# Last query block, page loads and weight splits: reordering around the attention of a two-layer decoder step

## What is computed

```
layer 0: h += hgrn2_mixer(rmsnorm(h)) @ w_o0 ;  h += conv_ffn(rmsnorm(h))
k, v, logf = shared_kv(h)           # keys and values of 16 heads of 64
layer 1: q, gate = split(rmsnorm(h) @ w_qg) ; q = rmsnorm(q) per head
         prompt:  p = softmax(q k^T / 8 + c_q - c_k, causal)        # 512 x 512 per head
         samples: the same over 512 cached keys (4 pages of 128) and the 8 new ones
         h += (p v * sigmoid(gate)) @ w_o1 ;  h += conv_ffn(rmsnorm(h))
```

## Time and profile before

| | |
|---|---|
| median of 3 runs | 1701.38 us (1699.66 to 1705.09) |
| profiled execution | 1702.34 us, its span 1700.8 us |
| TensorE busy | 1629.9 us, 96% |
| VectorE / ScalarE / GpSimd busy | 851.9 / 616.7 / 303.1 us |
| mean granted TensorE clock | 0.981 of full speed |

### The profile page before, as it was taken

The page is one execution under the profiler, slowest core; times in us unless marked ns, Lnnn a source line. Parts: engine busy times, 40 slices in busy tenths (PEclk is TensorE's granted clock), DMA queues, the critical chain, the costliest instruction groups (busy, mean ns, idle before and its releaser), DMA issues.

```text
span 1700.8 us, 36540 instructions
## 1 busy us (share of the span) xinstructions
PE 1629.9 (96%) x14346; PEld 1554.1 (91%) x14346; DVE 851.9 (50%) x1498; ACT 616.7 (36%) x978; POOL 303.1 (18%) x363
## 2 busy tenths in 40 slices
PE   5999999979999999999999999888899999999997
PEld 5998989959999999999999999655699999999997
DVE  5666666644555555433343443566455555554221
ACT  4444334423333333322233354556334333333111
POOL 3222222212222222100100100122022222221000
PEclk8999999989999999999999999999999999999999
DMA  4222222212222222222233334388422222223330
GB/s 171 64 90 83 74 88 77 79 40 87 85 81 86 77 83 80 86 84 80 85 114 114 117 107 146 106 320 312 179 87 89 77 84 86 75 85 93 99 99 30
DMA packets 51879, 174.41 MB, mean 103 GB/s; under 512 B 6914, under 2 KB 8338, under 8 KB 51778
## 3 DMA queue, kind: packets, MB, share of 16 engines
q1 hardware_dynamic: 46850, 155.83, 27.7%
q0 software_dynamic: 4928, 17.12, 2.8%
HBM read 160.36 MB, written 12.57 MB: 102 GB/s over the span
## 4 chain that ended last, share of the span: by engine, by line
PE 71%; issue 3%; DVE 2%; ACT 1%; DMA 1%; SPq 0%; POOL 0%; DVEq 0%; ACTq 0%; POOLq 0%
PE acc L1450 66%; DMA dec_B<-c_samp 1%; PE aux L1631 1%; PE aux L1697 1%; PE aux L1752 1%; PE aux L1710 1%; PE acc L1729 1%; PE acc L1680 0%; ACT att_Pr L694 0%; SPq L374 0%; DVE w_lo L779 0%; PE aux L1494 0%; DVE att_Pr L1169 0%; ACT w_hi L433 0%; DVE acc L1156 0%
## 5 line engine op out<-in xcount | busy, mean ns | idle before, releaser
L1450 PE MATMUL acc<-xl,w_hi 128*128 128x288 f32 x2192 | 489.6, 305 | 23.4 <-DVE w_lo L779 14.7
L1450 PE MATMUL acc<-xh,w_lo 128*128 128x288 f32 x2192 | 473.6, 298 | 0.0
L1450 PE MATMUL acc<-xh,w_hi 128*128 128x288 f32 x2192 | 473.4, 298 | 0.0
L779 DVE TENSOR_TENSOR w_lo<-w_raw,w_hi 128x1024 fp32r<-128x1024 f32 (+1 forms) x217 | 283.6, 1307 | 331.9 <-ACT w_hi L433 330.4
L1450 PEld LDWEIGHTS acc<-xl,w_hi 128*128 128x128 f32 x2192 | 356.6, 191 | 35.2 <-DVE w_lo L779 15.4
L1450 PEld LDWEIGHTS acc<-xh,w_hi 128*128 128x128 f32 x2192 | 357.4, 191 | 0.0
L1450 PEld LDWEIGHTS acc<-xh,w_lo 128*128 128x128 f32 x2192 | 357.1, 191 | 0.0
L433 ACT ACTIVATE w_hi<-w_raw 128x1024 fp32r<-128x1024 f32 (+1 forms) x217 | 224.4, 1034 | 268.3 <-PE acc L1450 235.4
L1450 PE MATMUL acc<-ffn_glo,w_hi 128*128 128x288 f32 x704 | 151.3, 296 | 0.0
L1450 PE MATMUL acc<-ffn_gh,w_lo 128*128 128x288 f32 x704 | 150.0, 293 | 0.0
L1450 PE MATMUL acc<-ffn_gh,w_hi 128*128 128x288 f32 x704 | 149.1, 293 | 0.0
(11 more groups left out here) (241 smaller groups left out, 2102.9 us busy)
## 6 DMA issues: line engine op xcount, KB each, us to landing
w_raw<-w_fi_in SPq DMA_DIRECT2D x88, 512.0 KB, 3.3
w_raw<-w_mix_in SPq DMA_DIRECT2D x32, 512.0 KB, 3.3
w_raw<-w_fo_in SPq DMA_DIRECT2D x32, 512.0 KB, 3.5
dec_Kd<-cache_k_in SPq DMA_DIRECT2D x32, 512.0 KB, 5.8
att_Vd<-cache_v_in SPq DMA_DIRECT2D x32, 512.0 KB, 5.8
w_raw<-w_kv_in SPq DMA_DIRECT2D x17, 512.0 KB, 3.4
w_raw<-w_o_in SPq DMA_DIRECT2D x16, 512.0 KB, 3.3
w_raw<-w_qg_in SPq DMA_DIRECT2D x16, 512.0 KB, 3.3
```

Of the source, the lines that this page charges most:

```text
L779: nc.vector.tensor_tensor(w_lo[:, pos.slot % SPL, 0:width], w_raw[:, pos.slot, 0:width], w_hi[:, pos.slot % SPL, 0:width].bitcast(F32), AL ...
L1450: mm = nc.tensor.matmul(acc[:, tp, hf, 0:HALF], W[:, sp_, 128 * (j0 + j):128 * (j0 + j) + 128], X[:, kt, HALF * hf:HALF * hf + HALF], star ...
```

## The change

- **Splits.** In the `w_o0`/`w_o1` loop of `ffn`, `hi` and `lo` of block m+2 are done in round m: on ScalarE ahead of the tile's square and `xh`, on VectorE between `add_h` and `gain_lo`.
- **First scores.** `score(0, 0)` is issued within the last gate block, after its third k-tile. VectorE does its two `mx`, `inverse` and `scale_p` ahead of the scaling of gate tile 7; ScalarE does its two `ex` within `key_norm` of query tile 7.
- **Late norm.** `key_gain` of query tile 7 stands behind `mx` of tile 1 in round 0; the gate logarithm of tile 7 comes later, after `ex` of tile 1. In round 0 `turns(0, 0)` stands ahead of `score(0, 1)`.
- **Memory.** `Kd` changes places with `Pr` and `PT`. So the key pages of sample 0 are loaded only when block 140 is done, behind the loads of `w_o1` blocks 0 to 3.
- **Block 142.** Its `hi` and `lo` move from round 0 to the end of round 7.
- **End.** `sample_scores(7)` comes after round 7, `turns(7, 2)` and `sample_turn(6)` are in round 7 and no longer within the first `w_o1` block; `sample_max(7)` and `sample_exp(7)` move behind round 7.

```diff
         t3 = Region("dec", x_at)
-        Kd = t3("Kd", [P, PAGES, 8 * P])
+        Pr = t3("Pr", [P, 2, 2, SEQ])
+        PT = t3("PT", [P, 2, 2, NCH, P])
...
         t4 = Region("att")
-        Pr = t4("Pr", [P, 2, 2, SEQ])
-        PT = t4("PT", [P, 2, 2, NCH, P])
+        Kd = t4("Kd", [P, PAGES, 8 * P])
...
             sample_bias(0)
-            key_pages(0)
             for j in range(4):
                 load(Pos(B_WO1 + j), d["w_o1"][j])
             sp.wait_ge(block_done, B_WO1)
+            key_pages(0)
             value_pages(0)
...
                 for m in range(DT):
-                    if m:
-                        hi(Pos(b_in - 8 + m + 1))
+                    hi(Pos(b_in - 8 + m + 2))
                     out_tile(m, n_h0 + m + 1, None, s_base + m, G_FFN + 8 * layer)
-                hi(Pos(b_in + 1))
...
                 if split is not None:
                     hi(split)
+                if between is not None:
+                    between()
                 act.wait_ge(km_ps, n + 1)
...
+            def first_ex():
+                ex(0, 0, 0)
+                ex(0, 0, 1)
             qg_pair(0, 6, 3, 4)
-            qg_pair(1, 7, 3, 4, True)
+            qg_pair(1, 7, 3, 4, True, first_ex)
...
                     ex(i, 1, 1)
+                    if not prev:
+                        gate_log_of(7)
                     ex(i, 2, 0)
                     ex(i, 3, 0)
...
-                    ex(3, 1)
-                    if not prev:
-                        hi(Pos(B_WO1 + 1))
+                    ex(i, 3, 1)
                 if i == NSEQ - 1:
-                    sample_exp(i)
+                    hi(Pos(B_WO1 + 1))
...
                 for m in range(DT):
-                    if m:
-                        lo(Pos(b_in - 8 + m + 1))
                     add_h(m, b_in - 8 + m, (t_in - 8 + m) % 2, h_base + m + 1)
+                    lo(Pos(b_in - 8 + m + 2))
                     gain_lo(xl, xh, m, G_FFN + 8 * layer, x_base + m)
-                lo(Pos(b_in + 1))
...
                 lo(Pos(B_QG + 2 + 2 * k, i, step))
+                if last is not None:
+                    last()
                 scaled(tile_of(GT, p), b + 1, (T_QG + 1) % 2, gx_ok)
...
+            def first_max():
+                mx(0, 0, 0)
+                mx(0, 0, 1)
+                inverse(0, 0, 1)
+                scale_p(0, 0, 0)
+                inverse(0, 1, 2)
+                scale_p(0, 0, 1)
...
                     mx(i, 1, 0)
                     mx(i, 1, 1)
                     if not prev:
-                        gate_logsig(7)
+                        key_gain(QT, 7, 15, gq[:, 0:1])
...
+            def first_score():
+                pe.wait_ge(kn_ok, 9)
+                score(0, 0)
...
                 if more:
                     pe.wait_ge(kn_ok, 16)
                     score(i + 1, 0)
-                else:
-                    sample_scores(i)
                 pv(i, 1)
-                if more:
-                    turns(i, 2)
-                    if prev:
-                        sample_turn(i - 1)
-            pe.wait_ge(kn_ok, 9)
-            score(0, 0)
+                turns(i, 2)
+                if prev:
+                    sample_turn(i - 1)
+            qg_pair(0, 6, 3, 4)
+            qg_pair(1, 7, 3, 4, {2: first_score})
             for i in range(NSEQ):
                 att(i)
             e = NSEQ - 1
-
-            def end_turns():
-                turns(e, 2)
-                sample_turn(e - 1)
+            sample_scores(e)
             pe.wait_ge(ex_ok, 8 * NSEQ)
             gemm(Pos(B_WO1), T_WO1, T_WO1 % 2, range(DT), ah, al, wait_x=(al_ok, 0), part=True, hfs=(0,),
-                 mid={0: end_turns, 2: lambda: pv(e, 2), 4: lambda: sample_turn_p(e)})
+                 mid={0: lambda: pv(e, 2), 4: lambda: sample_turn_p(e)})
```

More of the change, by code:

```diff
@@ L612, in _, with key_norm @@
             ffn(0, B_FI0, B_FO0, G_KV, 1, 0, 8)
-            def key_norm(src, p, n, split=None):
+            def key_norm(src, p, n, split=None, between=None):
                 act.wait_ge(kr_ok, n + 1)
@@ L666, in gate_exp, with qg_pair @@
                 nc.scalar.activation(tile_of(GT, p), tile_of(GT, p), ACT.Exp).then_inc(gt_ok, 1)
-            def qg_pair(k, p, i, step, last=False):
+            def qg_pair(k, p, i, step, last=False, between=None):
                 if isinstance(p, int) and p == 0:
@@ L672, in qg_pair @@
                 hi(Pos(B_QG + 2 + 2 * k, i, step))
-                key_norm(QT, p, p + 8, None if last else Pos(B_QG + 3 + 2 * k, i, step))
+                key_norm(QT, p, p + 8, None if last else Pos(B_QG + 3 + 2 * k, i, step), between)
                 if not last:
@@ L756, in att @@
                     gated_hi(i - 1)
+                    if not cur:
+                        sample_copy(i - 1)
                 else:
@@ L1110, in _, with qg_pair @@
             dve.wait_ge(gq_ok, 1)
-            def qg_pair(k, p, i, step, last=False):
+            def qg_pair(k, p, i, step, last=None):
                 b = B_QG + 2 * p
@@ L1125, in qg_pair @@
                 nc.vector.sem_inc(evac, 1)
-                if not last:
+                if last is None:
                     lo(Pos(B_QG + 3 + 2 * k, i, step))
-                key_gain(QT, p, p + 8, gq[:, 0:1])
-                if not last:
+                    key_gain(QT, p, p + 8, gq[:, 0:1])
                     gate_logsig(p)
@@ L1141, in _, with mx @@
                 qg_pair(1, 2 * i + 1, i, 4)
+            def mx(i, s, a):
+                x, w, at = tile_no(s, a), P * (NCH - s), tile_at(s)
+                dve.wait_ge(sc_ps, 3 * i + min(s, 2) + 1)
+                dve.wait_ge(msk_ok, 4 * i + (1, 3, 4, 4)[s])
+                nc.vector.sem_inc(taking, 1)
+                sc = acc[:, unit_bank(i, min(s, 2)), a, at:at + w]
+                bias = NC[:, i % 2, a, 0:w] if s < 3 else NC0[:, a, :]
+                nc.vector.tensor_tensor_reduce(out=sc, in0=sc, in1=bias, scale=-1.0, scalar=3.0e38,
+                                               op0=ALU.add, op1=ALU.min, accum_out=nm[:, x:x + 1]).then_inc(mx_ok, 1)
@@ L1142, in _ @@
+            def first_max():
[5 more added lines that the diff above has]
+                scale_p(0, 0, 1)
             qg_pair(0, 6, 3, 4)
-            qg_pair(1, 7, 3, 4, True)
+            qg_pair(1, 7, 3, 4, first_max)
             def att(i):
                 cur, prev = i < NSEQ, i > 0
[L1149 to L1167, removed]
-                    pr = Pr[:, n % 2, a, at:at + w]
-                    nc.vector.tensor_scalar(pr, pr, rr[:, x:x + 1], None, ALU.mult).then_inc(pn_ok, 1)
@@ L1216, in gate_sample @@
                     last.then_inc(dgo_ok, 1)
-                if cur:
-                    mx(0, 0)
-                    mx(0, 1)
-                    inverse(0, 1)
-                    scale_p(0, 0)
-                    if prev:
-                        sample_max(i - 1)
-                    inverse(1, 2)
-                    scale_p(0, 1)
+                if cur and prev:
+                    mx(i, 0, 0)
+                    mx(i, 0, 1)
+                    inverse(i, 0, 1)
+                    scale_p(i, 0, 0)
+                    sample_max(i - 1)
+                    inverse(i, 1, 2)
+                    scale_p(i, 0, 1)
+                if not cur:
+                    sample_max(i - 1)
                 if prev:
@@ L1765, in att @@
                     pv(i - 1, 2)
-                score(i, 1)
-                if not prev:
+                    score(i, 1)
+                    turns(i, 0)
+                else:
                     pe.wait_ge(kln_ok, 16)
-                turns(i, 0)
+                    turns(i, 0)
+                    score(i, 1)
                 score(i, 2)
```

85 lines of the change are left out of this document (45 added, 40 removed).

## The result

| | before | after |
|---|---|---|
| median beside each other, 5 runs each | 1702.41 us | 1690.82 us (1690.10 to 1692.34) |
| ratio, 95% interval | | 0.993 (0.9916 to 0.9945) |
| profiled execution, its span | 1702.34, 1700.8 us | 1692.34, 1690.8 us |

The forecast was 1692.0, in a range of 1687 to 1697.5, and "faster" at 0.84, with 0.3% as the bound; the whole interval of the ratio lies beyond it. The profiled execution of the changed kernel is the slowest of its five, 1.5 us over their median. It is 10.0 us shorter than the one before.

A forecast was written before the change was run, and what follows sets the result against it. TensorE, busy 96% of the span, was taken as the bound, so only its idle or slow spells could give. 3.0 + 1.3 + 2.0 + 3.5 = 9.8 us off 1702.34 or median 1701.38; forecast 1692.0, range 1687 to 1697.5.

The forecast's parts named there:

- Part 1a: Change-over into `w_o0`: splits first let block 34 start 2.0 us sooner, 1.0 less slow clock; 3.0 us (2.0 to 4.7).
- Part 1b: Layer 1's `w_o1` loop, before block 143: earlier splits remove TensorE's idle time; 1.3 us, lower end 1.0.
- Part 2: Into attention: moved halves of block 142 and first scores let `turns(0,2)` go sooner; 2.0 us, 0.3 to 2.9.
- the head start is used up: Into attention: late `key_gain` and the third mask hold `mx(0,2)` until 1087.6, against 1087.5 before.
- Part 3: End of attention: `pv(7,1)` and `turns(7,2)` run during the wait for `sample_scores(7)`; 3.5 us, 1.9 to 5.0.
- the two small waits: End of attention, new order: about 1.2 us until the copy of `turns(7,1)`, and 0.34 for the scaling before `turns`.
- A: Key pages land late, `sample_scores(0)` waits, all gain into attention goes; sum 7.8 us, or 1693.8; chance 0.12.
- B: End of attention gives only 0.5 us: clock drops again, value pages replace key pages; sum 6.8, or 1694.8; chance 0.09.
- C: Two more slow stretches at other moments in attention, each up to 1.65 us; sum 6.5, or 1695; chance 0.07.
- D: Masks and gate work hold `turns(0,2)`, attention's end waits as before; both attention gains are nothing, 1697.2; chance 0.06.
- E: Attention loop: late bias row brings three more 3.4 us stalls plus slow stretches, costing 15.2 us; 1707.7; chance 0.04.

The follow-up runs named there:

- run 2: Kernel before with only block 142's `hi` and `lo` moved from round 0 to the end of round 7: 1698.0 us, ratio 0.9982.
- run 10: Changed kernel with the old end of attention put back, measured again beside the changed kernel: 1691.7 us, ratio 0.9945 to before.
- runs 3 and 11: Changed kernel with the first scores put back behind the last gate block, measured twice: 1694.4 us (0.9958) and 1693.4 us (0.9951).
- 5: Kernel before with only the key pages of sample 0 issued later, behind the wait for block 140: 1701.8 us, ratio 1.0006.
- run 7: Changed kernel with two buffers for the samples' bias row, issued ahead of its sample's key pages: 1685.1 us, ratio 0.9906 to before.
- kernel 4: Changed kernel with the old end of attention put back: 1692.9 us, ratio 0.9961 to before.

## Why the prediction was right

**Part 1a** (3.0, 2.0 to 4.7): the 2.0 of the wait measured 2.0. Of the 2.7 of clock I credited 1.0; 2.5 came back, and in ten of the eleven profiles with the new splits block 34 runs at full clock. The term was mis-sized by 1.5, and I missed a second one of 1.5 at 862. The reason given for the 1.0 does not hold either: from 380.0 to 380.7 only 0.7 us of work would run before the drop, not 1.3, and the 1.3 us up to 382.0, idle before, would then be run slowly. Had the low clock stayed from 380.7 to 387.4, the part would have been about 1.4, below its lower end of 2.0. That it did not stay was not worked out; to that extent the term was luck. Alone the part is worth 6.1 us by the medians (4.1 to 8.7), where the prediction had 4.3 with 1b.

**Part 1b** (1.3): block 143 has no idle time in any kernel with the new order.

**Part 2** (2.0, 0.3 to 2.9): 3.3 in the profile, above the range. Of it 1.4 is the slow stretch behind `turns(0,2)`, for which 0.5 was credited. The order of events was as worked out, only earlier: counted from the end of the gate block, the third mask took 0.7 and not 1.3, and `turns(0,2)` came 0.7 sooner than forecast. Moving block 142 was priced at 1.5 and measured 2.1 of waits. The step "the head start is used up" held in waits (15.7 in run 2 without first scores, 15.4 to 15.8 with them) and failed for the clock: taking the first scores out of the changed kernel costs 2.9 us. They remove an idle spell at `turns(0,0)`, behind which the clock dropped in both profiles of it without them; the prediction looked only at `turns(0,2)` and at the spell before `turns(0,1)`. That one came as forecast, 3.1 us, but the slow stretch expected behind it came in none of eight profiles. No run varies the late norm or the places in memory by themselves.

**Part 3** (3.5, 1.9 to 5.0): 3.5 in this profile, with the two small waits at 1.09 and 0.40 where 1.2 and 0.34 were forecast. The six profiles with the old end say that the usual worth is 1.6 to 2.3 in waits, and run 10 that not all of it need be a wait for the key pages: the lower end was the sounder number, since I took a chance drop of the clock in one execution for a standing cost.

**The rivals.** A shows as 0.36 us in one of eight profiles. B is half right, by the lower worth of the end, but the clock dropped in none of the eight new ends. C came true in the loop, 3.1 us more slow clock there in this execution. D is refuted by the entry and the end. E did not come: still three bias stalls, 8.2 us against 8.6.

The rivals' times start from slightly different bases: taken from 1701.8, as the 1692.0 is, A to D come out 0.2 to 0.3 us higher, and E at 1707.2, not 1707.7. "Faster" does not depend on it.

So the sum of 9.8 met 10.0 between the profiled executions and 11.6 between medians (9.4 to 14.3 by the interval) because terms too small (the clock at block 34, at 862 and in the entry) made up for the slow clock in the loop and ahead of block 32. The waits of the named places were right to 0.6 us; that the total came so close is luck with the clock. As an estimate from these terms, a sum from the rows of one execution is good to 2 or 3 us here.

## What to carry to other kernels

Read a slow stretch in one profile as a chance with a price, and compare the same stretch in several executions before it is a term: the waits of the changed kernel repeated to 0.4 us or better between its two profiles, the clock behind them only in part. An idle spell on the busiest engine can be worth removing twice, for itself and for what may follow it: 4.8 us of entry in runs 3 and 11, nearly all of it clock. When a mask, or any small step, waits for a DMA, first look at what is queued behind it that does not need that DMA: moving one instruction in GpSimd's queue gave another 5 us on top of the change, as much as a second buffer did.

## What the runs showed of the hardware

**Slow stretches far apart came together.** The wait of 2.05 us for the low half near 857 is in all 14 profiles, but the clock drops behind it in only four. These are the four in which block 34, some 475 us earlier, runs at the low clock: before, 2, 5 and, in spite of the new splits, 7, where the window from 374 to 377, ahead of the wait, already reads 0.50. Windows of before, and of run 7:

```profile
862.00:865.30 3.30, 3.30 (x16) 3.30 (x15) 3.11 (x5) 0.68 (x1) 0.57 (x2) 0.50 0.46 172
```

```profile
380.40:386.00 5.60, 5.54 (x30) 5.55 (x31) 4.56 (x4) 2.28 (x3) 1.78 (x1) 0.68 0.58 181
858.00:862.00 4.00, 3.86 (x17) 3.86 (x18) 3.78 (x6) 1.12 (x2) 1.00 (x2) 0.57 0.44 143
```

In no profile does TensorE idle for as much as 0.4 us between the two places, so whatever shifts the work at the first shifts the second as well, and the clock may depend on that moment. That is an inference; no run shifted one place alone. The Trainium skill, "TensorE: Matmul & The Clock Gate", section "What's actually happening", says that the monitor runs freely and isn't started by the kernel, and the rows are compatible with it; they do not show it.

**One kernel, 13 us.** The ten runs of kernel 4 go from 1686.98 us (mean clock 0.987) to 1699.78 (0.978), and most of what lies between is ordered by that clock. Even the 372 us before the first edit lost about 11 to 19 us to it in the 14 profiles. What the loss at the start depends on stays open.
